# Gate and up of the feed-forward by seven half-size products in place of eight; the gated rows go out to HBM and come back for down

## The chip, the cores and the metric

One core of one Trainium2 chip runs the whole program. The time is the device time of one execution in microseconds, the median of several runs. The profile is one further execution, recorded by the hardware profiler. The core has a matmul engine (PE, with its weight loads shown as PEld), a vector engine (DVE), a scalar engine (ACT), a general engine (POOL, GpSimd) and an engine that issues transfers (SP).

## The reference, cut to what matters

The program is one step of a two-layer decoder trunk. A layer has a combined projection, four mixers, an output projection with a residual, and a gated feed-forward:

```
def residual_block(x, mix, w_out_l, g_ffn, wg, wu, wd):
    x = x + mix @ w_out_l
    h = rmsnorm(x, g_ffn)
    return x + (jax.nn.silu(h @ wg) * (h @ wu)) @ wd
```

x has 1024 prompt tokens and 8 x 4 sample tokens, together 1056, by D_MODEL = 1024, all float32. wg and wu are 1024 x 2816 and wd is 2816 x 1024. DEPTH is 2.

## The kernel before

Activations lie transposed: 128 partitions hold one row block of 128 features, and the 1056 tokens run along the free side (TT = 1056). D_MODEL is KR = 8 such row blocks and the hidden width is FR = 22. The tokens are taken in NCH = 3 chunks of CW = 352 columns. Every large product is done in a reduced float format of PE (fp32r) on operands that are split in a high and a low part, x = hi + lo. A product is then three passes: w_hi x_hi, w_hi x_lo and w_lo x_hi. All of them add up in one PSUM bank.

The feed-forward comes last in each layer. After the output projection the squares of the residual rows are summed (ACT squares them, DVE adds them up, PE sums over partitions) and ACT makes the inverse norm. `norm_split` on DVE then scales the rows chunk by chunk into `Hn`, ACT rounds them into `HNHR` (high) and DVE subtracts to get `HnR` (low). The hidden rows are worked in parts of PART = 6, 6, 6 and then 4. For one part, `ffn_part` on PE does for each of its rows r, and each of the 3 chunks, 24 matmuls of 352 columns for gate (`w_gate`) and 24 for up; L1261, L1263 and L1267 are the first product of a part, L1272, L1274 and L1276 the others. ACT takes Silu of the gate bank (L1788), DVE multiplies it with the up bank (L2420) and splits the result in `HDHR` and `HDLR`. Down follows in the same part: for each of 8 output row blocks m and 3 chunks it runs 3 x n matmuls (n = rows of the part), again at L1272, L1274 and L1276, and DVE adds the bank to the residual x (L2430). Nothing of the hidden rows leaves the chip's SBUF.

Weights come as jobs of 128 x 1024 floats (512 KB) for gate and up and 128 x 768 or 128 x 512 for down, through NSLOT = 4 slots `WS`. POOL issues the transfers (L513): a slot is loaded again when PE has done the product that used it. DVE splits each job (`split_weights`: a cast, L1910, and a subtraction, L1912) into `WHR` and `WSR`. POOL has no other work in the feed-forward. Order on each engine is the order of its code, and semaphores (`wait_ge`, `then_inc`) are the only link between engines.

## Time and profile before

| | |
|---|---|
| median of 3 runs | 3261.04 us (3261.03 to 3267.55) |
| span of the profiled execution, first to last instruction | 3272.9 us |
| PE busy | 3081.2 us, 94% of the span |
| PEld busy | 2866.7 us, 88% |
| DVE busy | 1877.2 us, 57% |
| ACT busy | 580.0 us, 18% |
| POOL busy | 419.5 us, 13% |
| mean granted PE clock | 0.961 of full speed |
| HBM traffic | 242.31 MB read, 50.74 MB written |

The profile gives no time of its own for the profiled execution beside its span; the span is 11.9 us over the median of the plain runs. Matmuls on PE are pipelined, so one lasts longer than the step from one start to the next; rates are read here from starts. "Idle before" is the time in which an engine stood still just ahead of an instruction, with what released it. Two instructions on one engine in a row of the timeline can be merged, with their count.

### The profile page before, as it was taken

The page shows a single profiled execution, that of the slowest core. Times are in us where ns is not written, and L with a number is a line of the kernel's source. Part 1 is how long each engine was busy: PE and PEld are TensorE (multiplying, and loading weights), DVE is VectorE, ACT ScalarE, POOL GpSimd, SP SyncE. Part 2 cuts the span into 40 slices and gives each one's busy share as a digit, 9 for nine tenths or more (in the row PEclk, how much of TensorE's full clock was granted, in tenths as well). Part 3 has the DMA queues.
Part 4 walks back from the last instruction along what each step waited for, and adds up shares of the span by engine and source line. Part 5 has one row for each costly group of instructions (what it writes and reads, how often), then busy time and mean ns, then how long its engine had stood idle before and what let it go on. Part 6 is the DMA issues. An engine that isn't in the chain of part 4 may idle for free.

```text
span 3272.9 us, 56197 instructions
## 1 busy us (share of the span) xinstructions
PE 3081.2 (94%) x21860; PEld 2866.7 (88%) x21876; DVE 1877.2 (57%) x3453; ACT 580.0 (18%) x1065; POOL 419.5 (13%) x594
## 2 busy tenths in 40 slices
PE   7899978999999999999979999789899999999997
PEld 6699965768899999999967999567698999999997
DVE  5798996595633333333448989875955333333335
ACT  3422122233200000000123122223412000000001
POOL 4154300000000000000041543000000000000000
PEclk9999989799999999999989999897999999999999
DMA  7354435231111111111142443443211111111112
GB/s 258 104 156 130 132 109 219 80 130 60 39 39 52 40 50 42 52 46 46 49 147 78 144 144 131 173 167 108 99 45 33 48 56 39 47 45 49 49 39 99
DMA packets 121143, 292.36 MB, mean 89 GB/s; under 512 B 19445, under 2 KB 70790, under 8 KB 116918
## 3 DMA queue, kind: packets, MB, share of 16 engines
q1 hardware_dynamic: 71938, 129.61, 11.4%
q0 software_dynamic: 33088, 102.84, 10.0%
q10 hardware_dynamic: 15844, 56.18, 4.9%
q8 instruction: 182, 2.98, 0.4%
q14 instruction: 91, 0.75, 0.1%
HBM read 242.31 MB, written 50.74 MB: 90 GB/s over the span
## 4 chain that ended last, share of the span: by engine, by line
PE 71%; DVE 18%; issue 5%; ACT 2%; POOLq 1%; DVEq 1%; DMA 1%; POOL 0%; ACTq 0%; SPq 0%
PE PS L1276 15%; PE PS L1274 15%; PE PS L1272 15%; DVE U L2012 10%; PE PS L934 6%; PE PS L1162 2%; PE PS L1298 2%; PE PS L1300 2%; PE PS L1299 2%; PE PS L948 2%; PE PS L858 1%; PE PS L880 1%; PE PS L899 1%; DVE U L2101 1%; PE PS L1263 1%
## 5 line engine op out<-in xcount | busy, mean ns | idle before, releaser
L2012 DVE TENSOR_SCALAR_CACHE_REDUCE U<-U,smu 32x2080 bf16<-32x2080 f32 (+6 forms) x462 | 504.8, 1146 | 13.7 <-issue 1.9
L2420 DVE TENSOR_TENSOR U<-PS,U 128x352 f32<-128x352 f32 x132 | 69.1, 523 | 535.9 <-ACT U L1788 535.8
L1276 PE MATMUL PS<-HNHR,WSR 128*128 128x352 f32 x1920 | 346.3, 322 | 0.0
L1274 PE MATMUL PS<-HnR,WHR 128*128 128x352 f32 x1920 | 345.3, 321 | 0.0
L1272 PE MATMUL PS<-HNHR,WHR 128*128 128x352 f32 x1920 | 345.3, 321 | 0.0
L1276 PEld LDWEIGHTS PS<-HNHR,WSR 128*128 128x128 f32 x1920 | 314.4, 188 | 0.0
L1272 PEld LDWEIGHTS PS<-HNHR,WHR 128*128 128x128 f32 x1920 | 313.6, 188 | 0.0
L1274 PEld LDWEIGHTS PS<-HnR,WHR 128*128 128x128 f32 x1920 | 313.6, 188 | 0.0
L513 POOL DMA_DIRECT2D WS<-wjobs x176 | 94.1, 535 | 1711.2 <-PE PS L1276 1469.6
L1788 ACT ACTIVATE U<-PS 128x352 f32<-128x352 f32 x132 | 61.5, 466 | 1344.6 <-PE PS L1276 1344.6
L1910 DVE CAST WHR<-WS 128x1024 fp32r<-128x1024 f32 (+2 forms) x152 | 94.5, 622 | 296.4 <-DMA WS<-wjobs 296.4
L1274 PE MATMUL PS<-HDLR,WHR 128*128 128x352 f32 x1056 | 200.7, 323 | 0.0
L1276 PE MATMUL PS<-HDHR,WSR 128*128 128x352 f32 x1056 | 200.6, 322 | 0.0
L1272 PE MATMUL PS<-HDHR,WHR 128*128 128x352 f32 x1056 | 200.5, 322 | 0.0
L543 POOL TENSOR_TENSOR WSR<-WS,HNHR 128x1024 fp32r<-128x1024 f32 x50 | 121.4, 2434 | 429.6 <-ACT HNHR L1411 429.6
L1276 PEld LDWEIGHTS PS<-HDHR,WSR 128*128 128x128 f32 x1056 | 175.2, 189 | 0.0
L1274 PEld LDWEIGHTS PS<-HDLR,WHR 128*128 128x128 f32 x1056 | 175.1, 188 | 0.0
L1272 PEld LDWEIGHTS PS<-HDHR,WHR 128*128 128x128 f32 x1056 | 174.8, 188 | 0.0
L1912 DVE TENSOR_TENSOR WSR<-WS,WHR 128x1024 fp32r<-128x1024 f32 (+2 forms) x152 | 165.0, 1085 | 11.4
L934 PE MATMUL PS<-XHR,HNHR 128*128 128x352 f32 x912 | 166.8, 325 | 0.0
L934 PE MATMUL PS<-XHR,WSR 128*128 128x352 f32 x912 | 165.1, 323 | 0.0
L934 PE MATMUL PS<-HnR,HNHR 128*128 128x352 f32 x912 | 164.9, 322 | 0.0
(299 smaller groups left out, 4854.3 us busy)
## 6 DMA issues: line engine op xcount, KB each, us to landing
WS<-wjobs POOLq DMA_DIRECT2D x113, 512.0 KB, 3.9
WS<-wjobs ACTq DMA_DIRECT2D x50, 512.0 KB, 4.4
WS<-wjobs POOLq DMA_DIRECT2D x48, 384.0 KB, 3.3
Hn<-ckT SPq DMA_DIRECT2D x16, 896.0 KB, 10.8
U<-kT_pool SPq DMA_DIRECT2D x160, 64.0 KB, 2.0
xres<-U SPq DMA_DIRECT2D x2, 4224.0 KB, 16.4
U<-xres SPq DMA_DIRECT2D x4, 2112.0 KB, 7.4
U<-v_pool SPq DMA_DIRECT2D x128, 64.0 KB, 2.4
```

What stands on the lines that cost most here:

```text
L513: pool.dma_start(slot(j % NJOBS, n), wjobs[bass.ds(L * NJOBS + j, 1), :, 0:n].rearrange("a p n -> (a p) n")).then_inc(w_in[j % NJOBS % NSL ...
L543: pool.tensor_tensor(out=WSR[:, j % NSLOT, 0:1024], in0=slot(j, 1024), in1=high_weights(a).bitcast(F32), op=ALU.subtract).then_inc(wp_lo, 1)
L934: m = mm(out, w[:, k * P:(k + 1) * P], x[:, k, t], start=n == 0 and k == 0, stop=n == 2 and k == KR - 1)
L948: m = mm(out, x[:, k, t:t + P], w[:, :, k * P:(k + 1) * P], start=n == 0 and k == 0, stop=n == 2 and k == KR - 1)
L1162: m = mm(blocks(PS[:, 2 * (s % 3) + a, i * n:(i + 1) * n], l), keys(l, a * 64, r)[:, t], queries(quer(l, a * 64, r)[:, t], l), start=True, ...
L1272: mm(out, w(k)[0], x(k)[0], start=k == 0, stop=False)
L1274: mm(out, w(k)[0], x(k)[1], start=False, stop=False)
L1276: i = mm(out, w(k)[1], x(k)[0], start=False, stop=k == n - 1)
L1910: v.tensor_copy(hi, x)
L1912: return tt(out=lo, in0=x, in1=hi.bitcast(F32), op=ALU.subtract)
L2012: ts(U[0:m, JUNK[i]:JUNK[i] + w // 2].bitcast(BF16), s, CANDF[0:m, i:i + 1], None, op, ALU.add, accum_out=into[0:m, i:i + 1])
L2420: tt(out=x, in0=PS[:, 2 * (t % 3) + 1, 0:CW], in1=U[:, SIL + (t % 3) * CW:SIL + (t % 3 + 1) * CW], op=ALU.mult)
```

## The change

Gate and up are computed by Strassen products in Winograd's form. The 1024 x 1056 input is cut in four quarters (`quad`: 4 row blocks by TH = 528 tokens), and so is the weight of a pair of hidden rows (4 row blocks by one hidden row). A pair of rows then takes NPROD = 7 products for gate and 7 for up in place of 8 and 8. A product is 4 row blocks x 3 passes x 2 halves of TQ = 264 tokens, 24 matmuls. There are NPAIR = 11 pairs. PE runs them in `gate_up(p)`, product number q = 14 p + 2 i + g, with i from 0 to 6 and g for gate or up.

- The sums of input quarters are made once per layer, in `norm_split` on DVE (three of 128 x 2112) and in `high_sums` on POOL (one). All seven inputs are then split: ACT rounds (`x_copy`), DVE subtracts (`low`), but for one, which POOL subtracts (`high_low`).
- The sums of weight quarters are made on POOL, eight subtractions or additions of 128 x 512 per pair (`weight_sums`). ACT rounds each of the 14 weight operands of a pair into a ring of three (`weight_high`), DVE subtracts (`weight_low`).
- The products accumulate in two pairs of banks, "A" and "C", for each of gate and up. ACT copies out three states of A (`snapshot`), DVE adds C to them (`add_snapshot`), ACT takes Silu, DVE multiplies (`hidden`).
- SP writes each pair of hidden rows to a new HBM tensor `hmid` (two stores of 128 x 1056 per pair). For down they are read back in PARTS of 4, 6, 6 and 6 rows (`hidden_rows`), and ACT and DVE split them (`hidden_high`, `hidden_low`) while the part before is on PE. `down(n)` runs four times after all of gate and up.
- The loops over parts are unrolled. Weight jobs are in a new order: all of gate and up first, then down.

The core of the diff:

```diff
+            def gate_up(p):
+
+                for q in range(14 * p, 14 * p + 14):
+                    i, g = (q - 14 * p) // 2, q % 2
+                    name, fresh = PRODUCTS[i]
+                    pe.wait_ge(wp_hi, W_HI + q + 1)
+                    if i == 0 and p:
+                        pe.wait_ge((f_silu, f_mul)[g], 4 * p)
+                    elif i == 1 and p:
+                        pe.wait_ge(wo_add, NCH * KR + 6 * p - 1 + g)
+                    elif i in (2, 4, 6):
+                        pe.wait_ge(un_ev, NUNIT + 6 * p + i - 1 + g)
+                    elif i == 3:
+                        pe.wait_ge(wo_add, NCH * KR + 6 * p + 1 + g)
+                    elif i == 5:
+                        pe.wait_ge(wo_add, NCH * KR + 6 * p + 3 + g)
+                    if p == 0 and g == 0:
+                        pe.wait_ge(x_hi, X_HI + i + 1)
+                    w_hi, w_lo = ring(q)
+                    for z in range(2):
+                        out, t = PS[:, BANK[name][g] + z, 0:TQ], slice(z * TQ, (z + 1) * TQ)
+                        for n, (w, x) in enumerate(((w_hi, x_high(i)), (w_hi, x_low(i)), (w_lo, x_high(i)))):
+                            if z == 0 and n == 1 and p == 0 and g == 0:
+                                if i == 4:
+                                    pe.wait_ge(fx_pool, 2)
+                                else:
+                                    pe.wait_ge(x_lo, X_LO + i + (i < 4))
+                            if z == 0 and n == 2:
+                                pe.wait_ge(wp_lo, W_LO + q + 1)
...
+            def weight_high(L, q):
...
+                if q >= 3:
+                    act.wait_ge(un_ps, NUNIT + q - 2)
...
+                copy(ring(q)[0], plain(p, i, g)).then_inc(wp_hi, 1)
...
+            def norm_split(L):
+
+                def low(i, src):
+                    v.wait_ge(x_hi, X_HI + i + 1)
+                    tt(out=x_low(i), in0=src, in1=x_high(i).bitcast(F32), op=ALU.subtract).then_inc(x_lo, 1)
...
+                b11, b12, b21, b22 = (quad(Hn, i) for i in range(4))
+                t2 = four(U, XLO[2])
+                v.wait_ge(nrm_inv, NCH)
+                for q in range(4):
+                    i = row_scale(q)
+                i.then_inc(fx_row, 1)
+                for q in range(4, 6):
+                    row_scale(q)
+                low(0, b11)
+                for q in range(6, 8):
+                    i = row_scale(q)
+                i.then_inc(fx_row, 1)
+                tt(out=b11, in0=b12, in1=b11, op=ALU.subtract).then_inc(fx_sum, 1)
+                low(1, b21)
+                weight_low(3)
+                v.drain()
+                tt(out=t2, in0=b22, in1=b11, op=ALU.subtract).then_inc(fx_sum, 1)
+                v.drain()
+                tt(out=b21, in0=b21, in1=t2, op=ALU.subtract).then_inc(fx_sum, 1)
+                low(2, t2)
+                weight_low(4)
+                low(3, b11)
+                gated(0, 2)
+                weight_low(5)
+                v.wait_ge(fx_pool, 1)
+                low(5, b22)
+                gated(0, 3)
+                weight_low(6)
+                gated(0, 4)
+                low(6, b21)
...
+                def hidden_rows(n):
+
+                    at, rows_ = PARTS[n]
+                    if n < 2:
+                        for half in range(2):
+                            sp.wait_ge(st_out[half], sent[half] + 16 * (NPAIR - 1 + n))
+                    sp.dma_start(down_plains(n), hmid[:, at:at + rows_, :]).then_inc((br_in, cr_in)[n % 2], 16)
```

What stands on PE behind the output projection, before (three of the 48 products of one part's first rows), where HNHR and HnR are the high and low input and WHR and WSR the weights:

```order
L747 MATMUL PS<-U,CT 128x352 x3
L1399 UNCONDITIONAL_BRANCH
L1399 ISA
L1329 ISA
L1336 ISA
L1261 MATMUL PS<-HNHR,WHR 128x352 x8
L1263 MATMUL PS<-HNHR,WSR 128x352 x8
L1267 MATMUL PS<-HnR,WHR 128x352 x8
```

The same place now, where XAR, XBR and HnR hold the seven inputs and RGR the ring of weights:

```order
L881 MATMUL PS<-U,CT 128x352 x3
L1454 MATMUL PS<-XAR,RGR 128x264 x144
L1454 MATMUL PS<-XBR,RGR 128x264 x4
L1454 MATMUL PS<-HnR,RGR 128x264 x4
L1454 MATMUL PS<-XBR,RGR 128x264 x8
```

The matmuls are 264 columns wide in place of 352, and there are 24 to a product.

What stands on DVE at the same place, before, from the last split of a weight job ahead of the norm to the first gated chunk:

```order
L1910 CAST WHR<-WS 128x1024
L1912 TENSOR_TENSOR WSR<-WS,WHR 128x1024
L1918 SCALAR_TENSOR_TENSOR Hn<-U,sm 128x352 x8
L1938 TENSOR_TENSOR HnR<-Hn,HNHR 128x4x352 x2
L1918 SCALAR_TENSOR_TENSOR Hn<-U,sm 128x352 x8
```

And now:

```order
L2139 SCALAR_TENSOR_TENSOR Hn<-U,sm 128x1056 x6
L2136 TENSOR_TENSOR XAR<-Hn,XAR 128x2112
L2139 SCALAR_TENSOR_TENSOR Hn<-U,sm 128x1056 x2
L2154 TENSOR_TENSOR Hn<-Hn 128x4x528
L2136 TENSOR_TENSOR XAR<-Hn,XAR 128x2112
L2180 TENSOR_TENSOR RGR<-WS,RGR 128x512
L2158 TENSOR_TENSOR U<-Hn 128x2112
L2160 TENSOR_TENSOR Hn<-Hn,U 128x4x528
L2136 TENSOR_TENSOR XAR<-U,XAR 128x2112
L2180 TENSOR_TENSOR RGR<-WS,RGR 128x512
L2136 TENSOR_TENSOR HnR<-Hn,XBR 128x4x528
L2191 TENSOR_TENSOR U<-PS,U 128x528
```

DVE now scales whole rows, and sums and splits quarters of 2112 elements between them.

On POOL there were only transfers (L513) at this place. Now the first pair reads so, and each later pair has eight of the additions and four transfers:

```order
L645 TENSOR_TENSOR WS<-WS 128x512 x5
L620 TENSOR_TENSOR Hn<-Hn 128x4x528
L645 TENSOR_TENSOR WS<-WS 128x512 x2
L626 TENSOR_TENSOR HnR<-Hn,XBR 128x4x528
L645 TENSOR_TENSOR WS<-WS 128x512
```

POOL computes there beside DVE, on tiles in SBUF, which it did not do before. Outside the feed-forward the order of all engines is as it was.

## Rows read from the trace of the kernel before

**Rows 1.** The page: engines, and the costliest group of matmuls.
```profile
PE 3081.2 (94%) x21860; PEld 2866.7 (88%) x21876; DVE 1877.2 (57%) x3453; ACT 580.0 (18%) x1065; POOL 419.5 (13%) x594
...
L1276 PE MATMUL PS<-HNHR,WSR 128*128 128x352 f32 x1920 | 346.3, 322 | 0.0
```

**Rows 2.** Timeline of PE in gate and up, then in down (start, length, instruction).
```profile
955.93 1.43 PE L1274 MATMUL PS<-HnR,WHR 128*128 128x352 f32 x8
...
1003.17 1.43 PE L1276 MATMUL PS<-HNHR,WSR 128*128 128x352 f32 x8
...
1596.57 0.81 PE L1272 MATMUL PS<-HDHR,WHR 128*128 128x352 f32 x4
...
1628.50 0.80 PE L1276 MATMUL PS<-HDHR,WSR 128*128 128x352 f32 x4
```

**Rows 3.** Timeline of PE in the combined projection, where the width changes.
```profile
232.89 1.46 PE L934 MATMUL PS<-XHR,WSR 128*128 128x352 f32 x8
234.19 1.11 PE L948 MATMUL PS<-HNHR,XHR 128*128 128x256 f32 x8
...
257.86 1.11 PE L948 MATMUL PS<-HNHR,HnR 128*128 128x256 f32 x8
```

**Rows 4.** Timeline of PE where the feed-forward begins, layer 0 and layer 1.
```profile
863.66 1.51 PE L1261 MATMUL PS<-HNHR,WHR 128*128 128x352 f32 x4 [6.88 <-ACT HNHR L1411]
865.55 1.54 PE L1261 MATMUL PS<-HNHR,WHR 128*128 128x352 f32 x4 [0.38 <-ACT HNHR L1411]
...
2484.99 1.51 PE L1261 MATMUL PS<-HNHR,WHR 128*128 128x352 f32 x4 [6.88 <-ACT HNHR L1411]
```

**Rows 5.** Windows there: stretch, length, busy times by engine, granted clock, transfers.
```profile
863.60:866.80 3.20, 2.76 (x8) 2.33 (x9) 3.20 (x3) 1.38 (x1) 0.00 (x0) 0.50 0.00 0
866.80:870.00 3.20, 3.20 (x17) 3.20 (x16) 3.20 (x7) 0.82 (x1) 0.00 (x0) 0.72 0.00 0
870.00:875.00 5.00, 5.00 (x33) 5.00 (x32) 5.00 (x7) 1.95 (x2) 0.00 (x0) 1.00 0.02 3
```

**Rows 6.** Timeline of ACT (inverse norm) and of DVE (row scaling) there.
```profile
859.50 1.27 ACT L1453 ACTIVATE U<-U 128x352 f32<-128x352 f32 x3
...
860.03 4.06 DVE L1918 SCALAR_TENSOR_TENSOR Hn<-U,sm 128x352 f32<-128x352 f32 x8 [2.26 <-ACT U L1453]
```

**Rows 7.** Groups of DVE and ACT in the feed-forward by shape: busy, mean ns.
```profile
L2420 DVE TENSOR_TENSOR U<-PS,U 128x352 f32<-128x352 f32 x66 | 34.6, 524 | 268.8 <-ACT U L1788 268.8
...
L1938 DVE TENSOR_TENSOR HnR<-Hn,HNHR 128x1408 fp32r<-128x1408 f32 x6 | 9.5, 1622 | 0.0
L1846 DVE TENSOR_TENSOR U<-U 128x1056 f32<-128x1056 f32 x6 | 7.6, 1258 | 1.0 <-issue 1.0
L1912 DVE TENSOR_TENSOR WSR<-WS,WHR 128x512 fp32r<-128x512 f32 x8 | 5.5, 692 | 0.6
...
L1433 ACT ACTIVATE U<-U 128x1056 f32<-128x1056 f32 x8 | 8.7, 1089 | 44.4 <-DVE U L2430 33.9 <-DVE U L2172 10.5
L1411 ACT ACTIVATE HNHR<-Hn 128x1408 fp32r<-128x1408 f32 x6 | 8.3, 1382 | 10.5 <-DVE Hn L1918 10.5
```

**Rows 8.** Timeline of DVE and POOL where both work on SBUF tiles, and POOL alone.
```profile
235.73 2.38 DVE L2050 SCALAR_TENSOR_TENSOR U<-U,smu 32x2080 f32<-32x2080 f32 x1
238.03 3.48 DVE L2066 TENSOR_TENSOR U<-U,CT 128x128 f32<-128x128 f32 x6
...
236.96 3.41 POOL L543 TENSOR_TENSOR WSR<-WS,HNHR 128x1024 fp32r<-128x1024 f32 x1 [0.26 <-ACT HNHR L1411]
...
265.01 2.34 POOL L543 TENSOR_TENSOR WSR<-WS,HNHR 128x1024 fp32r<-128x1024 f32 x1 [24.64 <-ACT HNHR L1411]
```

**Rows 9.** Transfers: count, KB each, median us from issue to landing.
```profile
WS<-wjobs POOLq DMA_DIRECT2D x113, 512.0 KB, 3.9
...
U<-xres SPq DMA_DIRECT2D x4, 2112.0 KB, 7.4
...
btok<-U ACTq DMA_DIRECT2D x12, 528.0 KB, 3.0
...
U<-btok SPq DMA_DIRECT2D x2, 3168.0 KB, 12.4
...
U<-ctok SPq DMA_DIRECT2D x2, 2112.0 KB, 17.2
```

More of the change, by code:

```diff
@@ new lines, in build, with plain, ring, quad @@
+        DN_BANKS = [(2, 3, 0), (1, 4, 5)]
+        def plain(p, i, g):
+            first, second = slot(J_GU + 4 * p + g, 1024), slot(J_GU + 4 * p + 2 + g, 1024)
+            return (first[:, 0:512], first[:, 512:1024], first[:, 0:512], second[:, 0:512], first[:, 0:512],
+                    first[:, 512:1024], second[:, 512:1024])[i]
+        def ring(q):
+            o = q % 3 * 1024
+            return RGR[:, o:o + 512], RGR[:, o + 512:o + 1024]
+        def quad(tile, i):
+            return tile[:, 4 * (i // 2):4 * (i // 2) + 4, i % 2 * TH:i % 2 * TH + TH]
@@ L442, in build, with down_high @@
+        def down_high(j, n):
+            o = DW_AT[(j - J_DN) % 4]
+            return split_cols(o, n * P)
+        ROWS_DONE = [sum(q[1] for q in PARTS[:n + 1]) for n in range(len(PARTS))]
         UNITS = [(0, i) for i in range(TILES)] + [(1, i) for i in reversed(range(TILES))]
@@ L558, in _ @@
                         (keys if call == "k" else values)(n, places)
[L559 removed]
+                for j in range(J_OUT + NSLOT, J_GU + NSLOT):
                     if j == J_OUT + NSLOT:
@@ L563, in _ @@
                             split_mix(k)
+                    load(j, job_floats(j), j - NSLOT)
+                for p in range(NPAIR):
+                    weight_sums(L, p)
+                    for j in range(J_GU + 4 * p + 4, J_GU + 4 * p + 8):
+                        load(j, job_floats(j), j - NSLOT)
+                for j in range(J_DN + NSLOT, NJOBS):
                     load(j, job_floats(j), j - NSLOT)
@@ L1398, in _ @@
                 norm_sums(0)
-                with pe.Fori(0, NPART) as f:
-                    ffn_part(f, PART)
-                ffn_part(NPART, LASTR)
+                for p in range(NPAIR):
+                    gate_up(p)
+                for n in range(len(PARTS)):
+                    down(n)
                 pe.drain().then_inc(layer_done, 1)
@@ new lines, in silu, with gates @@
+            def silu(p, q):
+                o = hblk(GB, (0, 3, 1)[q])
+                act.wait_ge(wo_add, NCH * KR + 6 * p + 2 * q + 1)
+                act.activation(o, o, ACT.Silu).then_inc(f_silu, 1)
+            def gates(L, p):
+                for n in range(14):
+                    q = 14 * p + n
+                    if n == 0:
+                        snapshot(p, 0, 0)
+                    elif n == 1:
+                        snapshot(p, 1, 0)
+                    elif n in (4, 5):
+                        snapshot(p, n - 4, 1)
+                    elif n in (8, 9):
+                        snapshot(p, n - 8, 2)
+                    elif n == 12:
+                        act.wait_ge(un_ps, NUNIT + 14 * p + 13)
+                        act.activation(wide(hblk(GB, 2)), banks("A", 0), ACT.Silu).then_inc(f_silu, 1)
+                    weight_high(L, q + 3)
+                    if p == 0 and n == 1:
+                        x_copy(2)
+                        x_copy(3)
+                    elif p == 0 and n == 2:
+                        x_copy(4)
+                    elif p == 0 and n == 3:
+                        x_copy(5)
+                        x_copy(6)
+                    if n in (2, 9, 11):
+                        silu(p, (2, 9, 11).index(n))
+                    if p == NPAIR - 1 and 6 <= n < 10:
+                        hidden_high(0, n - 6)
@@ L1941, in index_halves, with gated @@
+            def gated(p, n):
+                if n in (2, 3):
+                    add_snapshot(p, n - 2, 0)
+                elif n in (8, 9):
+                    add_snapshot(p, n - 8, 1)
+                elif n in (10, 11):
+                    add_snapshot(p, n - 10, 2)
+                if n == 4:
+                    hidden(p, 0)
+                elif n == 9:
+                    hidden(p, 1)
+                elif n in (12, 13):
+                    hidden(p, n - 10)
             def index_halves():
@@ L2432, in ffn_part @@
                             gather_tail(1, c, L)
-                    if n == LASTR and 2 <= m < KR - 1:
+                    if last and 2 <= m < KR - 1:
                         v.drain()
```

401 lines of the change are left out of this document (248 added, 153 removed).

## The prediction

> **What bounds the kernel now.** I read the page first, then the timeline of PE stage by stage, then what stands beside it. PE is busy 94% of the span [rows 1], but what counts is the spacing of its matmuls. In gate and up the timeline gives 296 matmuls of 352 columns from 955.93 to 1003.17, 159.6 ns each with nothing between them; in the last down part it is 200 from 1596.57 to 1628.50, 159.7 ns [rows 2]. The granted clock is 1.00 there, so the feed-forward runs at the 2.4 GHz level and PE alone sets its time. From the first matmul at 863.66 [rows 4] to the last start near 1629.1 (the row at 1628.50 holds four, 0.16 apart [rows 2]) it takes 765.5 us in layer 0. By the code that is 3168 matmuls for gate and up and 1584 for down; at 159.7 ns they make 758.9 us, and the other 6.6 go at the front, where PE waits and runs at the lower level (0.50 and 0.72 granted until 870 [rows 5]). Layer 1 starts at 2484.99 with the same wait, 6.88 us [rows 4]; I take it as equal. The other engines have room in the middle of this stage: DVE waited 268.8 us for ACT in the gated multiplies alone [rows 7].
>
> **What is removed and added on PE.** Per layer 3168 matmuls of 352 columns go and 11 x 14 x 24 = 3696 of 264 come. The columns fall to 7/8, but each matmul also has a part that does not shrink. The trace has no 264, but it has 256 and 352 side by side: 25 groups of 8 with 256 columns go from 234.19 to 257.86, 118.4 ns each, and the group of 352 just ahead takes 1.30 us, 162 ns [rows 3]. The line through both (0.45 ns a column) gives 122.0 ns at 264. Bounds are 118.4 below and 162 above; I take 122, which is 8 columns from a measured row. So a product takes 24 x 122 ns = 2.93 us, and 154 of them 450.9 us where before 3168 x 159.7 made 505.9. That is a gain of 55 us a layer if nothing waits. A full eighth would be 63.
>
> The Trainium skill ("TensorE: Matmul & The Clock Gate", section LDWEIGHTS) speaks against narrower matmuls: a weight load takes its column count over 1.2 GHz, 107 ns for 128 columns, and fp32 weights get no fast load. By that rule 264 columns would still cover the load, barely, and the sum would stay; the row at 256 columns agrees, being above that floor.
>
> **The front of a layer.** Here the change costs. Before, DVE scaled one chunk at a time and PE started 2.9 us after ACT's last inverse (859.50 + 1.27 = 860.77 [rows 6]; start 863.66 [rows 4]). Now PE needs whole quarters, and the first eight products (i = 0 to 3) are paced by one chain on DVE. I price it from shapes: a two-input DVE operation grows by (1622 - 1258) / 352 = 1.03 ns a column, so 2112 columns cost 2.35 us, about 2.30 from start to start; 1056 columns of scaling cost 1.21 (eight of 352 took 4.06 [rows 6], plus 704 x 1.03 ns); 512 columns cost 0.65 [rows 7]. Up to the weight low of product 7 DVE has 8 scalings (9.7), 6 lows and 3 sums of 2112 (20.7), 5 weight lows (3.3), two adds from PSUM of 528 (524 + 176 x 1.03 = 0.70 each, 1.4) and a multiply (0.6): 35.7 us. It also waits some 3 us for ACT, whose copies of 2112 grow by (1382 - 1089) / 352 = 0.83 ns a column to 1.97 us [rows 7] and stand in ACT's queue behind weight highs and snapshots. From 860.8 that would put product 8 at 860.8 + 38.7 + 2.0 (last 16 matmuls) = 901.5.
>
> **POOL in that chain.** POOL now computes on SBUF beside DVE, and the trace shows what this does. POOL's subtraction of 1024 columns takes 2.34 us alone (265.01). At 236.96 it meets a DVE instruction with two SBUF inputs and takes 3.41: its end, 240.37, less 2.34 is 238.03, the moment the DVE instruction ended. And DVE's next group, six tiny ones from 238.03, takes 3.48 us, so its first waited for POOL to end [rows 8]. Each engine holds the other off for a whole instruction. POOL's price is 2.34 / 1024 = 2.29 ns a column: 1.17 us for 512, 4.83 for 2112. In the chain stand two of 2112 (`high_sums`, `high_low`) and about six of 512 of which half fall into DVE's own waits: 9.7 + 3.5 = 13 us. That moves product 8 to 914.5, that is 50.8 us after 863.66. The lower clock after such waits (5 us of it before, [rows 5]) hides under the DVE chain. The Trainium skill has the same rule ("SBUF — State Buffer", Who interferes with whom): the two engines share one port pair, and a DVE instruction with two SBUF inputs contends with a GpSimd one that reads. With the rule and the rows the front costs 50.8; without holding off it would be 37.8.
>
> **The steady pairs.** PE's product takes 2.93 us. ACT per pair has 14 copies of 512 (about 0.6 by its shapes), 6 snapshots and 4 Silu, some 15 us of 41; DVE 14 weight lows, 6 adds, 4 multiplies, 16 us, and POOL 8 x 1.17 = 9.4. Even added up, DVE and POOL fill 26 of 41. The tightest order is product 10 behind `snapshot` and `add_snapshot` of product 8: 0.8 + 0.7 us of a slack of 2.93. The ring of three leaves two products, 5.9 us, for a copy and a subtraction of 1.3. A slot's transfer (3.9 us [rows 9]) is asked for some four products before its use, 11.7 us. I cost all of it at nothing; without that cover a late weight would cost up to 1.2 us (one POOL instruction) at a product. The stores of hidden rows (528 KB, 3.0 us [rows 9]) and the read of rows 0 to 3 (2112 KB, 7.4) lie under a pair.
>
> **Down.** 1584 matmuls of 352 stay, 1584 x 159.7 = 253.0. New is that rows 4 to 9 are asked for only when all of gate and up is done and its last store has landed: multiply 0.8, store 3.0, read of 3168 KB 12.4 [rows 9], ACT copy 1.1, DVE low 1.26 [rows 7], three adds 1.6, in all some 20.5 us. DVE waits for them in order behind the first output block, and PE may run three blocks ahead, 3 x 36 x 159.7 ns = 17.2 us, plus 0.3 at the start. So PE stands for 3 us there. Bounds: nothing, if the read is quicker; with a read as slow as the 17.2 us for 2112 KB [rows 9], 25.8 for 3168, it is 16.4. I take 3, by the row of the same size, and 0.5 for the last pair. Later reads start a whole part (69 us) ahead.
>
> **The sum.** Per layer 50.8 + 146 x 24 x 0.122 (427.5) + 253.0 + 3.0 + 0.5 = 734.8 against 765.5: 30.7 saved, 61.4 in both. Nothing outside the feed-forward is reordered. The profiled execution goes from 3272.9 to about 3211.5. Its own figure lies 11.9 above the median of the plain runs, so I subtract the 61.4 there too: 3261.0 - 61.4 = 3199.6, about 3200.
>
> **The rivals.**
> 1. POOL and DVE do not hold each other off here, or only in DVE's waits. For it: DVE has gaps. Against: [rows 8]. The front is 13 shorter, twice: 3200 - 26 = 3174.
> 2. Further waits in the front or at the seam to down, say the late read (13.4 more per layer) or a PE that stays at the lower level while it waits in pieces through the first pair (20 us at double time loses 10). That gives 3220 to 3227.
> 3. Slower, by one mechanism: each product's start is held by the hand-over ACT to DVE through the ring of three, because POOL's turns and the in-order queues of both make weight lows late. It decides at 61.4 / 292 = 0.21 us a product. At 0.3 it is 88 us, 3288. For it: ACT and DVE serve snapshots, adds and the ring in one queue each. Against: 5.9 us of slack and both engines under half full.
> 4. The seven products bring nothing: the 264-column matmul takes its time from something that does not shrink. It would need 131 ns in place of 122, and 256 columns take 118.4 in the trace. This gives 3261.
>
> **How the numbers follow.** Main case (3190 to 3210) 0.45, rival 1 0.17, rival 2 0.24, rival 3 0.08 and rival 4 0.03; 0.03 is for a weak form of rival 3 between 3232 and 3254. The range from 3168 to 3232 holds main, rival 1 and most of rival 2, 0.82. A measurement of this kernel tells 0.2%, 6.5 us, from no change. Faster by more than that: 0.90; same 0.03; slower 0.07.
>
> **What would show it.** Matmuls of 264 columns at 122 ns from start to start in the middle pairs, with PE's idle near nothing; if they stand at 131 or more, the gain is gone. Product 8 some 50 us after PE's first start of before; DVE instructions of 2112 columns lengthened by up to 4.8 us where POOL's `high_sums` and `high_low` stand, or at their plain 2.35 (rival 1). One PE wait of about 3 us in the fourth output block of the first down part. Waits of PE on weight lows in later pairs would make the prediction wrong towards rival 3.

## The result, and the profile after

The changed kernel takes 3210.97 us (median of 4 runs, 3209.38 to 3213.07) and the kernel before 3264.3 in the same comparison (4 runs, 3261.03 to 3273.03). The ratio on record is 0.9814, with a 95% interval of 0.9801 to 0.9828: faster by 1.9%. It is not the quotient of those two medians, which is 0.9837; four runs of a kernel that scatters by 12 us, as before does, make a poor median. The profiled execution spans 3211.4 us where before had 3272.9, so 61.5 us less. Nearly all of that lies in the stage that was changed: from DVE's last add of the output projection to the first matmul behind down it is 30.2 us in layer 0 (775.3 before, 745.1 now) and 30.5 in layer 1.

The page of the kernel after answers to [rows 1]: the engines, then two of the new matmul's groups and the new sums on POOL.
```profile
PE 2994.2 (93%) x22932; PEld 2774.9 (86%) x22932; DVE 2013.2 (63%) x3427; ACT 879.9 (27%) x1507; POOL 695.3 (22%) x774
...
L1454 PE MATMUL PS<-XAR,RGR 128*128 128x264 f32 x3168 | 404.6, 290 | 40.2 <-ACT XAR L1535 31.8
...
L645 POOL TENSOR_TENSOR WS<-WS 128x512 f32<-128x512 f32 x176 | 257.2, 1467 | 151.7 <-DVE RGR L2180 65.3
```
PE is 87 us less busy but the span is only 61.5 shorter. The 40.2 us of idle ahead of the first matmul group say where to look: two layers with some 20 us each, in which PE waits for a quarter of the activations.

PE's timeline from the start of layer 0's feed-forward, then at the seam to down (answers to [rows 4] and [rows 2]).
```profile
870.40 1.22 PE L1454 MATMUL PS<-XAR,RGR 128*128 128x264 f32 x4 [12.97 <-ACT XAR L1535]
873.04 13.77 PE L1454 MATMUL PS<-XAR,RGR 128*128 128x264 f32 x92 [1.42 <-DVE XAR L2136]
889.88 0.72 PE L1454 MATMUL PS<-XAR,RGR 128*128 128x264 f32 x4 [3.07 <-ACT XAR L1535]
893.40 8.02 PE L1454 MATMUL PS<-XAR,RGR 128*128 128x264 f32 x44 [2.80 <-DVE XAR L2136]
...
906.70 2.13 PE L1454 MATMUL PS<-XBR,RGR 128*128 128x264 f32 x8 [4.29 <-DVE RGR L2180]
...
913.75 1.15 PE L1454 MATMUL PS<-XBR,RGR 128*128 128x264 f32 x8
...
1343.02 1.46 PE L1476 MATMUL PS<-XAR,XBR 128*128 128x352 f32 x8
...
1361.17 1.54 PE L1476 MATMUL PS<-XAR,RGR 128*128 128x352 f32 x8 [0.71 <-DVE U L2703]
```
The five idle times at the head are the front. The last, 4.29 us, stands before the last 16 matmuls of product 6, and product 7 follows it without a wait. Product 8 begins with the fifth matmul of the group at 913.75, at 914.24. From there to down's first matmul at 1343.02 PE never waits, and at the seam it waits once, 0.71 us.

Windows of the kernel after: the pairs, then down (columns as in [rows 5]).
```profile
950.00:1200.00 250.00, 250.00 (x2045) 250.00 (x2044) 106.81 (x145) 85.83 (x147) 78.25 (x72) 1.00 0.23 78
1343.00:1590.00 247.00, 246.29 (x1534) 246.03 (x1533) 112.62 (x178) 24.41 (x24) 15.03 (x28) 1.00 0.24 85
```
PE is busy the whole 250 us at the 2.4 GHz level, and 250 / 2045 is 122.3 ns a matmul. DVE works 107 of 250, ACT 86, POOL 78.

DVE, then POOL, in the front of the kernel after.
```profile
860.67 10.05 DVE L2139 SCALAR_TENSOR_TENSOR Hn<-U,sm 128x1056 f32<-128x1056 f32 x6 [4.16 <-ACT U L1579]
...
880.80 6.94 DVE L2158 TENSOR_TENSOR U<-Hn 128x2112 f32<-128x2112 f32 x1
887.83 3.25 DVE L2160 TENSOR_TENSOR Hn<-Hn,U 128x2112 f32<-128x2112 f32 x1
891.00 2.35 DVE L2136 TENSOR_TENSOR XAR<-U,XAR 128x2112 fp32r<-128x2112 f32 x1
...
899.99 4.98 DVE L2136 TENSOR_TENSOR HnR<-Hn,XBR 128x2112 fp32r<-128x2112 f32 x1 [2.09 <-ACT XBR L1535]
```
```profile
880.78 4.74 POOL L620 TENSOR_TENSOR Hn<-Hn 128x2112 f32<-128x2112 f32 x1 [14.87 <-DVE RGR L2180]
885.48 3.38 POOL L645 TENSOR_TENSOR WS<-WS 128x512 f32<-128x512 f32 x1
...
897.99 4.77 POOL L626 TENSOR_TENSOR HnR<-Hn,XBR 128x2112 fp32r<-128x2112 f32 x1 [0.63 <-DVE RGR L2180]
```
This is the hand-over of [rows 8] in new places. POOL's sum of 2112 columns begins 0.02 us ahead of DVE's and holds it until 885.5, so DVE's operation shows 6.94 in place of 2.35. POOL's next, 1.27 us of work, is held in turn until DVE ends at 887.74 and shows 3.38; it ends at 888.86 and DVE's next, begun at 887.83, shows 3.25. Each waits until the other's instruction has ended. The second operation of POOL with 2112 columns starts at 897.99, 2 us ahead of DVE's at 899.99, which therefore waits for the rest of it only and shows 4.98.

### The profile page after: what moved, and what is told of

Its sections match the earlier page's. It is cut to its first block, busy times and chain, and to the rows that moved or that the text cites. A ratio compares the mean times of both kernels' runs of the same rounds, so it can differ in the third digit from the quotient of the medians.

```text
span 3211.4 us, 58867 instructions
## 1 busy us (share of the span) xinstructions
PE 2994.2 (93%) x22932; PEld 2774.9 (86%) x22932; DVE 2013.2 (63%) x3427; ACT 879.9 (27%) x1507; POOL 695.3 (22%) x774
## 3 DMA queue, kind: packets, MB, share of 16 engines
q0 software_dynamic: 33088, 102.84, 10.5%
## 4 chain that ended last, share of the span: by engine, by line
PE 69%; DVE 20%; issue 4%; ACT 2%; DMA 2%; DVEq 1%; POOLq 1%; POOL 0%; SPq 0%; ACTq 0%
PE PS L1454 27%; PE PS L1476 15%; DVE U L2292 10%; PE PS L1068 7%; PE PS L1296 2%; PE PS L1403 2%; PE PS L1405 2%; PE PS L1404 2%; PE PS L1082 2%; PE PS L992 1%; PE PS L913 1%; PE PS L1014 1%; PE PS L1033 1%; DVE U L2381 1%; DVE U L2398 1%
## 5 line engine op out<-in xcount | busy, mean ns | idle before, releaser
L1454 PE MATMUL PS<-XAR,RGR 128*128 128x264 f32 x3168 | 404.6, 290 | 40.2 <-ACT XAR L1535 31.8
L1454 PEld LDWEIGHTS PS<-XAR,RGR 128*128 128x128 f32 x3168 | 400.9, 193 | 42.7 <-issue 33.2
L2180 DVE TENSOR_TENSOR RGR<-WS,RGR 128x512 fp32r<-128x512 f32 x308 | 238.2, 775 | 288.5 <-ACT RGR L1535 287.8
L1454 PE MATMUL PS<-XBR,RGR 128*128 128x264 f32 x2816 | 409.8, 287 | 8.5 <-DVE RGR L2180 8.5
L1454 PEld LDWEIGHTS PS<-XBR,RGR 128*128 128x128 f32 x2816 | 371.8, 190 | 8.9 <-DVE RGR L2180 8.9
L1535 ACT ACTIVATE U<-PS 128x528 f32<-128x528 f32 (+12 forms) x338 | 166.1, 502 | 568.6 <-PE PS L1454 253.7
L645 POOL TENSOR_TENSOR WS<-WS 128x512 f32<-128x512 f32 x176 | 257.2, 1467 | 151.7 <-DVE RGR L2180 65.3
L1535 ACT ACTIVATE RGR<-WS 128x512 fp32r<-128x512 f32 x308 | 193.0, 628 | 276.9 <-PE PS L1454 276.9
L1454 PE MATMUL PS<-HnR,RGR 128*128 128x264 f32 x1408 | 229.5, 285 | 0.0
L1454 PEld LDWEIGHTS PS<-HnR,RGR 128*128 128x128 f32 x1408 | 197.0, 190 | 0.0
## 6 DMA issues: line engine op xcount, KB each, us to landing
Hn<-ckT SPq DMA_DIRECT2D x16, 896.0 KB, 10.7
Hn<-hmid SPq DMA_DIRECT2D x4, 3168.0 KB, 11.5
```

Source lines behind the costliest of these rows:

```text
L645: pool.tensor_tensor(out=plain(p, to, g), in0=plain(p, a, g), in1=plain(p, b, g), op=op).then_inc(fw_sum, 1)
L1454: m = mm(out, w[:, k * P:(k + 1) * P], x[:, k, t], start=fresh and n == 0 and k == 0, stop=n == 2 and k == 3, skip_group_check=True)
L1535: return act.activation(out, in_, ACT.Copy)
L2180: tt(out=lo, in0=plain(p, i, g), in1=hi.bitcast(F32), op=ALU.subtract).then_inc(wp_lo, 1)
```

## The experiments

All are timed against the kernel before, and the ratio carries its 95% interval. To compare fronts I use one interval that no other stage disturbs: from DVE's last add of the output projection (853.69 in the kernel after) to the start of product 8 (914.24). In the kernel after it is 60.55 us. The runs differ by up to some 6 us in when this stage begins, which the interval leaves out. The last column does the same for all of gate and up: from DVE's last add to down's first matmul, both layers together.

| run | median us | ratio | span us | last add to product 8, layer 0 | last add to down, both layers |
|---|---|---|---|---|---|
| the changed kernel | 3210.97 | 0.9814 [0.9801, 0.9828] | 3211.4 | 60.55 | 978.6 |
| e0_same | 3209.51 | 0.9813 [0.9796, 0.9831] | 3207.3 | 60.55 | 978.7 |
| e1_dve_sums | 3199.84 | 0.9779 [0.9765, 0.9793] | 3200.2 | 55.35 | 968.1 |
| e2_pool_idle | 3187.66 | 0.9740 [0.9724, 0.9755] | 3186.6 | 49.37 | 957.1 |
| e3_order | 3185.17 | 0.9742 [0.9728, 0.9755] | 3182.6 | 47.90 | 957.2 |
| e4_pool_twice | 3221.64 | 0.9852 [0.9836, 0.9868] | 3219.5 | 67.26 | 992.1 |
| e5_widths | 3162.78 | 0.9676 [0.9660, 0.9693] | 3157.3 | | 936.6 |
| e6_dve_weight_sums | 3182.79 | 0.9725 [0.9708, 0.9743] | 3178.6 | 46.02 | 952.2 |
| e7_eight | 3333.52 | 1.0188 [1.0171, 1.0205] | 3339.4 | | 1107.3 |
| e8_w128 | 3211.99 | 0.9820 [0.9784, 0.9856] | 3199.8 | | 970.0 |
| e9_low6_later | 3179.61 | 0.9721 [0.9705, 0.9737] | 3171.1 | 45.5 | 949.1 |

**e0_same** is the changed kernel again.

> The changed kernel once more, unchanged, beside the kernel before on one chip. Both theories: product 8 of layer 0 starts near 914.2 us, and the plain runs lie within 0.2% of 3211. It shows how far the plain runs of the kernel before spread (so far 3261.0 to 3273.0), which decides whether the gain is 53 or 61.

It gave 0.9813 and the same 60.55 us to the hundredth: in these two profiles the front repeats. The nine runs of before beside it lay between 3266.58 and 3274.47.

**e1_dve_sums**: the two operations of 2112 columns move from POOL to DVE.
```diff
-                            if p == 0 and n == 2 and g == 1:
-                                high_sums()
-                            if p == 0 and n == 3 and g == 1:
-                                high_low()
...
                 weight_low(3)
+                tt(out=quad(Hn, 1), in0=b22, in1=quad(Hn, 1), op=ALU.subtract).then_inc(fx_pool, 1)
...
-                v.wait_ge(fx_pool, 1)
+                v.wait_ge(x_hi, X_HI + 5)
+                tt(out=x_low(4), in0=quad(Hn, 1), in1=x_high(4).bitcast(F32), op=ALU.subtract).then_inc(fx_pool, 1)
```


> The sum and the subtraction of 2112 columns that POOL does in the front of a layer are done by DVE, at the same places of its order. Theory (POOL and DVE hold each other off for whole instructions): DVE gains more than it takes on, 4.6 us that its sum t2 was held and 2.6 of the low of input 5, against 2.3 for the new sum, while the new low falls into a wait of 2.1. Product 8 starts 4.9 us sooner, near 909.3, and the time falls by some 10 us. Rival (POOL worked free of charge beside DVE, and the long DVE instructions have another cause): two more DVE instructions of 2.3 us stand in the chain, product 8 starts 2.5 us later, and the time grows by 5 us.

DVE's timeline there in e1_dve_sums.
```profile
881.48 2.35 DVE L2153 TENSOR_TENSOR Hn<-Hn 128x2112 f32<-128x2112 f32 x1
883.92 3.27 DVE L2155 TENSOR_TENSOR U<-Hn 128x2112 f32<-128x2112 f32 x1
887.29 2.36 DVE L2157 TENSOR_TENSOR Hn<-Hn,U 128x2112 f32<-128x2112 f32 x1
```
DVE does 4.7 us more work and the front is 5.2 us shorter; the median is 9.7 below that of e0_same beside it, for two layers. By the lengths in the kernel after (6.94 and 4.98, where 2.36 is the plain length) the two operations on POOL held DVE for 7.2 us and saved it 4.7. The net is more than the difference of these two, since DVE's new low part stands where DVE had waited 2.09 us for ACT, and since PE's last 40 matmuls ahead of product 8 take 6.4 us in place of 7.5, more of them at the higher clock level. The middle one above still loses 0.9 to a weight sum of 512 columns on POOL.

**e2_pool_idle**: the same, and in the first pair POOL's weight sums are cut from 512 to 16 columns. It leaves out most of those sums, so that POOL hardly touches SBUF in the front.
```diff
+                            cut = 16 if p == 0 else 512
+                            pool.tensor_tensor(out=plain(p, to, g)[:, 0:cut], in0=plain(p, a, g)[:, 0:cut],
+                                               in1=plain(p, b, g)[:, 0:cut], op=op).then_inc(fw_sum, 1)
```


> As the run before, and POOL's eight weight sums of the first pair are cut to 16 of 512 columns (the products of that pair are then of wrong weights; all else is computed), so POOL does next to nothing in the front. Theory: DVE's first six scalings take 7.3 us and not 10.05, and 1.2 + 0.9 + 0.5 + 0.45 us go elsewhere; product 8 starts some 6 us before that of the run before, near 903.4, and the time is 22 us under the changed kernel's. Rival: product 8 where the run before has it.

DVE's timeline there in e2_pool_idle.
```profile
860.08 7.46 DVE L2136 SCALAR_TENSOR_TENSOR Hn<-U,sm 128x1056 f32<-128x1056 f32 x6 [4.94 <-ACT U L1576]
...
877.45 2.35 DVE L2154 TENSOR_TENSOR Hn<-Hn 128x2112 f32<-128x2112 f32 x1
879.89 2.36 DVE L2156 TENSOR_TENSOR U<-Hn 128x2112 f32<-128x2112 f32 x1
882.34 2.36 DVE L2158 TENSOR_TENSOR Hn<-Hn,U 128x2112 f32<-128x2112 f32 x1
```
The six scalings take 7.46 us in place of 10.05, the three below them stand at their plain length, and the front is 6.0 us shorter again, 11.2 in all. The median is 21.9 below that of e0_same, for two layers.

**e4_pool_twice** goes the other way: POOL does each weight sum twice, in every pair.
```diff
+                            pool.tensor_tensor(out=plain(p, to, g), in0=plain(p, a, g), in1=plain(p, b, g), op=op)
+                            pool.drain()
                             pool.tensor_tensor(out=plain(p, to, g), in0=plain(p, a, g), in1=plain(p, b, g), op=op
```


> POOL makes every weight sum twice (16 operations of 512 columns in a pair; the sums that are then taken of sums are wrong, and nothing else changes). Theory (the steady pairs have room: DVE and POOL together fill 26 us of a pair's 41, and would fill 36): PE stands nowhere after product 8; the front grows by what POOL holds DVE off once more, some 6 us a layer, so the time grows by about 12 us, to 3222. Rival (the ring of three and the queues of ACT and DVE leave little slack): PE waits in each pair, 1 us or more, and the time grows by over 30.

The window of the pairs in e4_pool_twice.
```profile
950.00:1200.00 250.00, 250.00 (x2045) 250.00 (x2044) 128.29 (x146) 85.90 (x146) 155.93 (x123) 1.00 0.23 78
```
POOL's busy time doubles (156 in place of 78) and DVE's grows from 107 to 128 by being held off, yet PE still starts 2045 matmuls in 250 us. PE waits for nothing from product 8 to down. In the front the same doubling costs 6.7 us, and the ratio is 0.0038 higher, 12 us for two layers, which is about that front twice. The same contention is free in the pairs and paid in the front. This also disposes of rival 3: with POOL's turns twice as long the hand-over through the ring is still in time.

**e3_order** keeps e1's move and changes the order: the products of the front no longer wait behind work that only later ones need. ACT's copies 4 to 6 are issued at products 4 to 6, DVE makes the sum that is input 4 after the weight low of product 6 and its low part after that of product 7, and the low parts of inputs 5 and 6 come behind the weight lows of products 8 and 9.
```diff
-                    elif p == 0 and n == 2:
-                        x_copy(4)
-                    elif p == 0 and n == 3:
-                        x_copy(5)
-                        x_copy(6)
+                    elif p == 0 and 4 <= n < 7:
+                        x_copy(n)
...
+                tt(out=quad(Hn, 1), in0=b22, in1=quad(Hn, 1), op=ALU.subtract).then_inc(fx_pool, 1)
                 gated(0, 4)
+                weight_low(7)
+                v.wait_ge(x_hi, X_HI + 5)
+                tt(out=x_low(4), in0=quad(Hn, 1), in1=x_high(4).bitcast(F32), op=ALU.subtract).then_inc(fx_pool, 1)
+                weight_low(8)
+                low(5, b22)
+                weight_low(9)
                 low(6, b21)
```


> The two POOL operations of 2112 columns go to DVE, and what the first eight products don't need goes behind them: the sum and low of input 4 and the lows of inputs 5 and 6 stand behind the weight lows of products 6 and 7, and ACT's copies of inputs 4, 5 and 6 come with products 4, 5 and 6. Theory (the front is one chain on DVE): product 8 starts near 899.5 in place of 914.2, and both layers together save about 29 us, to some 3182. Rival (ACT's copies or the lower PE clock set the front): less than 8 us in all.

PE's timeline in the front of e3_order.
```profile
866.07 1.22 PE L1450 MATMUL PS<-XAR,RGR 128*128 128x264 f32 x4 [13.00 <-ACT XAR L1531]
868.71 14.22 PE L1450 MATMUL PS<-XAR,RGR 128*128 128x264 f32 x96 [1.42 <-DVE XAR L2129]
884.73 3.81 PE L1450 MATMUL PS<-XAR,RGR 128*128 128x264 f32 x28 [1.79 <-DVE XAR L2129]
889.30 2.22 PE L1450 MATMUL PS<-XAR,RGR 128*128 128x264 f32 x16 [0.76 <-DVE RGR L2178]
...
904.90 0.73 PE L1450 MATMUL PS<-XBR,RGR 128*128 128x264 f32 x4 [1.28 <-ACT RGR L1531]
```
The first two waits stand as they were. The next three (3.07, 2.80 and 4.29 in the changed kernel) shrink to 1.79 and 0.76, at the price of a new one of 1.28 before product 10. The front is 12.65 us shorter, where 14.7 was expected, and some of that is lost again before product 10: to down's first matmul it is 10.7 a layer. The median is 24.3 below that of e0_same. Of the 12.65, e1's move made 5.2 and the order 7.45, with POOL's weight sums left where they are; an idle POOL with the old order gave 6.0 on top of e1. Whether the two add up no run shows. DVE's timeline of e3 still has the six scalings at 10.08 us and one sum at 3.49 in place of 2.35, so there is holding off left that the order didn't remove.

**e6_dve_weight_sums**: e3, and the first five weight sums go to DVE, which stands idle there for ACT's inverse.
```diff
+                            if p == 0 and 2 * n + g < 5:
+                                continue
...
+                for n, (to, a, b, op) in enumerate(((3, 6, 3, ALU.add), (2, 3, 0, ALU.subtract), (5, 1, 2, ALU.subtract))):
+                    v.drain()
+                    for g in range(2 if n < 2 else 1):
+                        if n == 0:
+                            loaded(v, L, J_GU + 2 + g)
+                        tt(out=plain(0, to, g), in0=plain(0, a, g), in1=plain(0, b, g), op=op).then_inc(fw_sum, 1)
```


> The reordered front of the run before last (order), and the first five weight sums of a layer are made by DVE in the 4 us in which it waits for ACT's inverse norm, in place of POOL between 854 and 866 us. Theory (POOL holds DVE off): the adds of the norm and the first six scalings lose the 1.2 and 2.8 us for which POOL held them; 4 us a layer, 8 in all, to a ratio near 0.9717 where the reordered front had 0.9742. Rival: DVE has five more instructions and nothing to gain, no change or slower.

DVE's timeline ahead of its row scaling, in e6_dve_weight_sums.
```profile
853.02 2.86 DVE L2144 TENSOR_TENSOR WS<-WS 128x512 f32<-128x512 f32 x4 [1.97 <-DMA WS<-wjobs]
855.80 7.45 DVE L2134 SCALAR_TENSOR_TENSOR Hn<-U,sm 128x1056 f32<-128x1056 f32 x6
```
The six scalings take 7.45 us in place of 10.05, but they now start 7.22 us after the last add (848.58) where they started 6.98 after it: the last load of weights came late and DVE's sums behind it reached past ACT's inverse. The front is 1.9 us shorter than e3's where 4 was expected, and 2.5 a layer to down's first matmul; in the medians the two can't be told apart.

**e9_low6_later**: e6, with the last activation low moved behind the weight low of product 11 (issued at product 8).
```diff
-                low(6, b21)
...
+                        if p == 0 and n == 8:
+                            v.wait_ge(x_hi, X_HI + 7)
+                            tt(out=x_low(6), in0=quad(Hn, 2), in1=x_high(6).bitcast(F32), op=ALU.subtract).then_inc(x_lo, 1)
```


> The reordered front with the five weight sums on DVE, and the low of input 6, first needed by product 12, goes behind the add that product 10 waits for. Theory: the 1.1 us for which PE stood before product 10 go in both layers, 2 us in all, to a ratio near 0.972 of the kernel before; less than the measurement tells, so the trace decides. Rival: the wait moves to another product.

PE's wait before product 10 (1.28 us in e3, 1.14 in e6) is gone, and so it had been DVE's queue. This version has the lowest median of those that compute everything; its ratio is 0.0093 below the changed kernel's, 30 us, and the last column of the table has 29.5. Its margin over e3 and e6 in plain time is within their intervals.

**e5_widths**: is the time of a narrow matmul its columns? The three terms of a product (high by high, high by low, low by high), all of 264 columns in the changed kernel, get 264, 192 and 128. The columns beyond are left out.
```diff
+                            c = (TQ, 192, 128)[n]
+                            t = slice(z * TQ, z * TQ + c)
...
-                                m = mm(out, w[:, k * P:(k + 1) * P], x[:, k, t], start=fresh and n == 0 and k == 0,
+                                m = mm(out[:, 0:c], w[:, k * P:(k + 1) * P], x[:, k, t], start=fresh and n == 0 and k == 0,
```


> In gate and up the second pass of each product (high weights, low inputs) is 192 columns wide and the third 128 in place of 264, so part of each product is left out; the number of matmuls and weight loads stays. Theory (a fixed part of about 12 ns and the columns over 2.4 GHz): 92 ns at 192 and 65 ns at 128 from start to start, a product of 8 x 122 + 8 x 92 + 8 x 65 = 2.23 us and some 200 us less, if ACT and DVE keep up. Rival (the weight load of 128 columns is a floor at 107 ns, as the page on TensorE in the Trainium skill has it): both passes stand at 107 ns, a product takes 2.69 us, and the time falls by about 70.

The window of the pairs in e5_widths.
```profile
950.00:1200.00 250.00, 250.00 (x2166) 250.00 (x2165) 113.90 (x156) 90.68 (x155) 83.78 (x78) 1.00 0.26 88
```
250 / 2166 is 115.4 ns a matmul, not the 93 or so that the columns alone would give: 7 ns less than with 264 throughout, by 7008 matmuls in two layers 49 us. Both layers are 42.0 us shorter to down's first matmul; of the rest a part goes at the end of the front, where the granted clock is 0.50 until about 914. PE waits for no other engine in the pairs, so neither ACT nor DVE holds the rate. The line through 256 and 352 columns would reach 115.4 at about 249 columns; the mean doesn't follow it further down.

**e8_w128** tests whether that is a floor: the widths 264, 128 and 128, 256 columns fewer still in each twelve matmuls.
```diff
-                            c = (TQ, 192, 128)[n]
+                            c = (TQ, 128, 128)[n]
```


> As the run with two widths, but the second and third pass are both 128 columns wide, so eight matmuls of 128 follow each other in each half product (part of each product is left out; the number of matmuls and weight loads stays). There a group of four 192 wide took 106 ns each. Theory now (the weight load of 128 columns is a floor near 107 ns under every matmul of this form): the matmuls of 128 that follow one of 128 stand at about 107 ns too, and a product takes near 2.7 us. Rival (the cost goes on falling with the width, and what held the last run was the change of widths): 65 to 80 ns, and a product under 2.3 us.

Windows of e8_w128: the front, two stretches behind it, and the pairs.
```profile
900.00:925.00 25.00, 23.60 (x110) 23.41 (x109) 11.91 (x12) 5.38 (x10) 4.89 (x4) 0.50 0.15 43
925.00:940.00 15.00, 15.00 (x71) 15.00 (x71) 5.70 (x7) 2.94 (x6) 5.04 (x5) 0.50 0.32 107
940.00:950.00 10.00, 10.00 (x58) 10.00 (x57) 2.05 (x4) 2.06 (x4) 2.54 (x2) 0.61 0.13 54
950.00:1200.00 250.00, 250.00 (x2166) 250.00 (x2165) 112.96 (x154) 90.34 (x154) 83.38 (x75) 1.00 0.23 78
```
The last window counts 2166 matmuls, just as e5's: 11% fewer columns bring nothing. So the mean of weight load and matmul stands on a floor of about 115 ns for these widths, and PE waits for no engine here either. The Trainium skill ("TensorE: Matmul & The Clock Gate", section LDWEIGHTS) gives a weight load its column count over 1.2 GHz, which for 128 columns makes 107 ns; it does not call that a floor, and the mean of the rows is 8 ns above the figure. PE's weight side is busy 250 of 250, but so it is in the changed kernel at 122.3 ns; what points at the loads is the spacing of their starts, in the last section. The median (3211.99, of only two runs, 3201.50 and 3222.48) is nevertheless that of the changed kernel, and the reason for most of it is told there too.

**e7_eight** gives the saving back: one product in seven is done twice, so that eight are run on the new machinery.
```diff
-                    for z in range(2):
+                    for z in (0, 1) * (2 if i == 6 else 1):
```


> PE runs the last of the seven products of each pair twice, for gate and for up, so it runs 16 products where the changed kernel has 14 and the plain form would have 16 (the last product counts double in the result). Both theories of the front agree here: if PE alone sets the steady pairs, 11 x 2 x 2 more products of 2.94 us make 129 us, to 3340, which is 75 over the kernel before: the price of narrower matmuls and of the front without the eighth. If PE waited anywhere in the pairs for others, it would be less than 129.

The product that is run twice counts double in the result, so this kernel computes something else and serves for its time alone. The span is 128.0 us above the changed kernel's, and 128.7 by the last column, where 22 products a layer at 24 x 122.4 ns make 129. So a product more costs its full time, and one less brings it. It also prices the rest of the change: with all eight products its span is 66.5 us above that of before (3339.4 against 3272.9) and its ratio 1.9% above one. That is the price of narrower matmuls, front and seam, which the product left out must first pay. The narrower matmuls alone are 22 of it: 4224 at 122.4 ns a layer against 3168 at 159.7.

## Why the prediction was right, step by step

**The sum.** All times are of layer 0.

| step | predicted | measured |
|---|---|---|
| front, 863.66 to product 8 | 50.8 (914.5) | 50.6 (914.24) |
| 146 products | 427.5 at 122.0 ns | 428.8 (1343.02) at 122.4 ns |
| stall at the seam | 3.0 | 0.71 |
| down with the seam, first to last start | 256.5 | 255.2 |
| both layers, in the profiled execution | 61.4 less | 61.5 less (60.7 from last add to the end of down) |

Three readings in the working are slightly off and change nothing: the last start before is 1628.98 by its row and not 1629.1, the terms named for the late read add to 20.2 and not 20.5, and a scaling of 1056 columns is 1.23 by its own terms and not 1.21 (e2 has 1.24).

**The matmul of 264 columns** came within 0.4 ns of the line through 256 and 352. That choice was sounder than its reason: e5 and e8 show that the mean does not fall far below there. At 264 columns it is 122.4, at 256 118.4 [rows 3], and then 115.4 for both mixes of narrower ones. Rival 4 (131 ns) fell with it.

**Holding off in the front.** The kind was right, as e1 and e2 show, and rival 1 fell. The size of 13 us came out right too, by two errors that offset. Read from the lengths on DVE in the kernel after against those in e2, the two operations of 2112 columns held it for 7.2 us, where 9.7 was priced: the second was 2 us under way before DVE came. The weight sums held it for 5.6, where 3.5 was priced: 2.6 in the six scalings, 1.2 in the adds ahead of them (2.38 for two of 352 columns, 1.17 in e2), 0.9 in one sum and 0.9 in two weight lows. Together it is 12.8, of which 11.6 lie in the chain that the sum is about. The Trainium skill's rule on the shared port pair ("SBUF — State Buffer", Who interferes with whom) is that a DVE instruction with two SBUF inputs contends with a GpSimd one that reads SBUF; the timeline after agrees, with 6.94 us in place of 2.36 where both meet.

**The end of the front.** That product 8 came at 914.24 for 914.5 is partly two errors that cancel. My sum ended with the weight low of product 7 at 912.5 and 2.0 us for the 16 matmuls behind it. In the kernel after, DVE's timeline has the weight lows of products 6 and 7 (two in the last row) as follows.
```profile
905.51 1.13 DVE L2180 TENSOR_TENSOR RGR<-WS,RGR 128x512 fp32r<-128x512 f32 x1
...
909.63 1.28 DVE L2180 TENSOR_TENSOR RGR<-WS,RGR 128x512 fp32r<-128x512 f32 x2
```
The one of product 7 is done at 910.3, 2.2 us earlier than summed, and PE did not wait for it. The chain was the 35.7 of work as summed, 2.1 of waiting for ACT (3 were priced) and 11.6 of holding off (13), 49.4 in place of 51.7; by the timeline it took 49.6. PE's last wait ended with the one of product 6, at 906.64. From there it had 40 matmuls to do before product 8 and took 7.54 us for them where 122.4 ns each make 4.9: that the lower clock hides under the DVE chain failed for these, by 2.6 us. Windows of the kernel after show the clock behind each wait.
```profile
870.40:873.00 2.60, 1.22 (x4) 0.91 (x4) 2.60 (x3) 0.00 (x0) 0.00 (x0) 0.50 0.00 0
873.00:886.90 13.90, 13.77 (x92) 13.56 (x92) 13.78 (x6) 5.60 (x7) 6.12 (x2) 0.81 0.01 1
...
893.40:902.00 8.60, 8.60 (x51) 8.60 (x51) 6.51 (x5) 5.70 (x6) 7.25 (x2) 0.69 0.00 0
...
906.70:910.00 3.30, 3.30 (x15) 3.30 (x16) 3.27 (x3) 0.00 (x0) 0.00 (x0) 0.50 0.00 0
```
A granted clock between 0.50 and 1.00 is a window with both levels in it. PE is at the 1.2 GHz level three times, each time behind a wait: from 870.4, from 893.4 and from 906.7. What it loses the first two times does hide, since it waits for DVE again at 886.8 and at 902.4; the third time nothing is late behind it.

**What the chain needed.** "Paced by one chain on DVE" was right, but part of the chain was order and not need: e3 took 12.65 us out, 7.45 of it by order alone, with every operation still done. The order of instructions shows this without a run. I had summed the chain and not asked which links product 8 needs.

**The pairs at nothing.** There is no PE idle from 914 to 1343, and e4 shows that even with POOL's work doubled there would be none. The cover is real and wide, and rival 3 fell.

**The seam.** 3.0 against 0.71. The kernel after shows store and read in its transfers (count, KB, median us to landing), and then ACT's first copy of what was read:
```profile
hmid<-U SPq DMA_DIRECT2D x44, 528.0 KB, 2.6
...
Hn<-hmid SPq DMA_DIRECT2D x4, 3168.0 KB, 11.5
...
1357.25 5.96 ACT L1535 ACTIVATE XBR<-Hn 128x1056 fp32r<-128x1056 f32 x6 [16.34 <-DMA Hn<-hmid]
```
The store took 2.6 us in place of 3.0. The read in question was issued at 1346.71 and had landed when ACT began at 1357.25, 10.5 us in place of 12.4; 11.5 is the median of all four. The two make 2.3 us, about the whole difference. DVE also waited for a load of weights there, until 1357.36, so a faster read alone would not have shortened its queue.

A slow read as in rival 2 did not come, and neither did a clock that stays low through the first pair: it is at 1.00 from 914.3. Rival 2 was closest to true in the 2.6 us above.

**The plain time.** Here one term was off, the base. I took the 61.4 from 3261.0, the median of three runs, and the forecast of 3199.6 came out 11.4 low; 3210.97 is 1 us outside the band of the main case, although the main case is what happened. The 11.9 us between the profiled execution and that median were not a cost of profiling: in every comparison above the profiled execution is one of the plain runs, and its span is 1.6 to 2.0 us less than its time (3211.4 and 3213.07 here). The kernel before scatters, with medians from 3264.3 to 3273.06 over the comparisons, and 3272.9 was one of its longer executions. Less 61.4, the medians of nine runs (3267.93 to 3273.06) give 3206.5 to 3211.7.

## What to carry to other kernels

Price an algorithm that saves an eighth of the products from its parts: here the product left out saved 128 us (e7), and 66.5 of it went into matmuls whose fixed part does not shrink, 22, and into a front where whole quarters must be ready and the seam. Before helping DVE from POOL, ask whether DVE has slack there: on DVE's critical chain two operations of 2112 columns cost 7.2 us of holding off and saved 4.7, while the contention of the weight sums, doubled, was free behind 250 us of solid matmuls. And before moving work, list which links of the chain the next product really needs: the order alone was worth 7.45 us of front, and an idle POOL 6.0.

## What the runs showed of the hardware

**A floor for a weight load with its matmul.** With 264, 192 and 128 columns the mean is 115.4 ns, with 264, 128 and 128 it is 115.4 as well. The starts are not even, though. PE's timeline of e8_w128 (each row is named by its first shape) has:
```profile
1001.80 0.56 PE L1456 MATMUL PS<-HnR,RGR 128*128 128x128 f32 x4
1002.20 1.16 PE L1456 MATMUL PS<-XBR,RGR 128*128 128x128 f32 x8
1003.19 0.56 PE L1456 MATMUL PS<-HnR,RGR 128*128 128x128 f32 x4
```
The four of 128 in the first row take 0.40 us, 100 ns each. The eight behind them are four of 128 and four of 264 and take 0.99, 124 each. The weight loads that belong to them are even, as PEld's timeline of the same run shows:
```profile
1001.68 0.53 PEld L1456 LDWEIGHTS PS<-HnR,RGR 128*128 128x128 f32 x4
1002.14 1.00 PEld L1456 LDWEIGHTS PS<-XBR,RGR 128*128 128x128 f32 x8
1003.07 0.54 PEld L1456 LDWEIGHTS PS<-HnR,RGR 128*128 128x128 f32 x4
```
Four take 0.46 us and eight 0.93, 115 and 116 ns each, whatever the width of the matmul beside them. That speaks for the loads keeping the pace here, with the matmuls falling in behind. It is a reading and not shown: a run with 128 columns throughout, or with one load for several matmuls, would settle it, and there is none.

**A stream without gaps that stays at the lower level.** In e8_w128 PE is busy 15.00 of 15.00 us from 925 to 940 at a granted clock of 0.50, and since 870.83 it had waited only once, 1.40 us ahead of 904.39; only about 947 does the clock rise to 1.00. In e5_widths, whose only difference is 192 columns in place of 128 in one of the three passes, the window answering to it is at the 2.4 GHz level, although PE there had waited 3.62, 2.31 and 4.60 us in its front:
```profile
925.00:940.00 15.00, 15.00 (x133) 15.00 (x132) 7.50 (x9) 5.56 (x10) 10.48 (x8) 1.00 0.26 102
```
Layer 1 repeats it, 0.50 from 2480 to 2520 in e8_w128 against 1.00 in e5_widths. The counts are 71 matmuls against 133. From the last add to down's first matmul e8 is 33.4 us longer than e5 over both layers; the other 9 of the 42.5 in the spans lie in other stages, which scatter from run to run. So narrow matmuls behind a front can cost more clock than they save columns. I have seen it with these two widths alone, in one profile of each, and no run shows why.

**A front that repeats.** The changed kernel run twice gave the same 60.55 us from DVE's last add to product 8, though the stage began 3.4 us apart in the two. From last add to down's first matmul the two profiles have 489.33 and 489.34 us in layer 0, and 489.27 and 489.33 in layer 1. Changes of 2 us can be read there from one profile where the plain medians, which scatter by several us, show nothing.
